# The gate and up products of both Swiglu layers by Strassen's recursion, seven products of 256 tokens in place of eight

## The chip, the cores and the metric

The kernel runs on one core of a Trainium2 chip. Its time is device microseconds (us) of one launch. All tensors are float32.

## The reference

Three blocks of different make follow one another on 512 tokens of width 1024 (a Mamba-2 block with an MLP, a block with RWKV-7 and sliding attention between two Swiglu layers, and a block with spatial gating, forgetting attention and convolutional feed-forward layers). The change is about the two Swiglu layers of the second block:

```
D_MODEL, SEQ, D_FF_2 = 1024, 512, 2816

def rms_norm(x, g, eps=RMS_EPS):
    y = xf * lax.rsqrt(jnp.mean(xf * xf, axis=-1, keepdims=True) + eps)
    return y * g

def swiglu(h, w_gate, w_up, w_down):
    return (jax.nn.silu(h @ w_gate) * (h @ w_up)) @ w_down

def second_block(x, ...):
    x = x + 0.5 * swiglu(rms_norm(x, ffn1_norm[l]), ffn1_w_gate[l], ffn1_w_up[l], ffn1_w_down[l])
    ...  # the two mixers
    x = x + 0.5 * swiglu(rms_norm(x, ffn2_norm[l]), ffn2_w_gate[l], ffn2_w_up[l], ffn2_w_down[l])
    return rms_norm(x, final_norm[l])
```

## The kernel before

Activations lie transposed, features on the 128 partitions and the 512 tokens along the free side, in blocks of 128 features: `resid` has 8 blocks, the hidden layer of a Swiglu 22. All matrices go through one pipeline, the class `Flow`. It cuts its matrices into **steps** of at most 128x1024 weights, numbered through in `Flow.steps`. A step's weights are loaded by SyncE into one of four ring slots (`RING`); the load of step g waits until TensorE is through with step g-4. ScalarE rounds them into a high part (`split_high`), VectorE subtracts it from the whole and gets the low part (`split_low`), and TensorE makes three products for each 128x128 tile of weights: high weights by low activations, low by high, high by high (`multiply`). The semaphore `products` counts what TensorE has done, `emptied` counts the banks of its results that were taken.

A Swiglu has three matrices. Gate and up have 22 steps each. A step is one output block: 8 tiles, 3 products each, 24 matmuls of 512 tokens. Down has 8 output blocks of 22 tiles, 528 matmuls. VectorE takes a gate block from its bank and multiplies it with the factor of the norm (`rg.factor`, L2257), ScalarE applies Silu (L2238); VectorE multiplies the up block with it (L2269), ScalarE rounds the hidden block (L2243), VectorE makes its low part (L2273). The order of work on each engine is the order in which `Swiglu.tensor`, `scalar` and `vector` issue it; each engine keeps to its order and halts at a wait, with all that stands behind it. GpSimd does nothing in this stage. `Handoff` makes the high and low parts of the activations ahead of the first matrix, from each finished block of `resid`.

In the profile's rows all weight and activation memory is called `arena`, and L1317 and L1325 are the lines of `split_high` and `split_low`, L1377 is TensorE's in `multiply`, and L1280 is SyncE's load. The first Swiglu (`middle_bank`) runs its gate and up from about 1274 to 1516 us, the second (`later_bank`) from about 2143 to 2390 us.

## Time and profile before

| | us |
|---|---|
| three runs | 3604.70, 3606.09 (the median), 3608.92 |
| span of the profiled execution | 3608.4 |
| TensorE busy | 3540.6 |
| VectorE busy | 2041.9 |
| ScalarE busy | 1534.2 |
| GpSimd busy | 322.6 |

The span goes from the first to the last instruction of one execution that was profiled. It has no time of its own beside its span here, and lies among the three runs. Busy times are shares of different stages, so what a change in one stage is worth has to be read from that stage.

### The profile page before, as it was taken

How to read it: one execution, taken by the hardware profiler on the slowest of the kernel's cores; microseconds unless marked ns; L12 is line 12 of the kernel's file. 1: busy time of each engine (PE TensorE's matmuls, PEld its weight loads, DVE VectorE, ACT ScalarE, POOL GpSimd, SP SyncE). 2: the span in 40 equal slices, each digit the busy share in tenths (PEclk: the TensorE clock that was granted, in tenths of full speed). 3: DMA queues.
4: the chain of work that ended last, by engine and by line, in shares of the span. 5: the costliest groups of instructions: out<-in, count | busy, mean ns of one | idle time of the engine just before them, and what ended most of it. 6: DMA issues, size and time to landing. Idle time of an engine off the chain costs nothing. (4 is left out here: it accounts for less than half of the span.)

```text
span 3608.4 us, 49456 instructions
## 1 busy us (share of the span) xinstructions
PE 3540.6 (98%) x20379; PEld 2918.3 (81%) x20379; DVE 2041.9 (57%) x2881; ACT 1534.2 (43%) x2459; POOL 322.6 (9%) x307
## 2 busy tenths in 40 slices
PE   8999999999999999999999999999999999999998
PEld 6888788888788888887778778888988887877887
DVE  5987687775534454446686663444364744355743
ACT  5674678543423332222553432233353323275322
POOL 3772000000000000002111000000000000043000
PEclk9999999999999999999999999999999999999999
DMA  6345644333333333333320233333223333411332
GB/s 204 99 135 172 200 129 144 113 95 94 88 94 99 94 94 100 96 94 96 95 76 3 77 100 95 98 94 105 88 82 94 97 97 94 139 50 51 96 96 86
DMA packets 597624, 365.34 MB, mean 101 GB/s; under 512 B 16887, under 2 KB 578887, under 8 KB 596887
## 3 DMA queue, kind: packets, MB, share of 16 engines
q1 hardware_dynamic: 592807, 350.43, 32.8%
q10 hardware_dynamic: 4592, 11.73, 0.8%
q8 instruction: 162, 2.65, 0.3%
q14 instruction: 63, 0.52, 0.1%
HBM read 345.70 MB, written 15.89 MB: 100 GB/s over the span
## 5 line engine op out<-in xcount | busy, mean ns | idle before, releaser
L1377 PE MATMUL later_bank<-arena 128*128 128x512 f32 (+1 forms) x6792 | 1435.6, 373 | 9.8 <-DVE arena L1325 6.6
L1377 PEld LDWEIGHTS later_bank<-arena 128*128 128x128 f32 x6792 | 1193.2, 188 | 246.0 <-DVE arena L1325 14.3
L1317 ACT ACTIVATE arena<-arena 128x1024 fp32r<-128x1024 f32 (+3 forms) x545 | 566.4, 1039 | 1529.4 <-PE later_bank L1377 751.0
L1377 PE MATMUL middle_bank<-arena 128*128 128x512 f32 x4896 | 1125.5, 391 | 1.9 <-DVE arena L1325 1.1
L1377 PEld LDWEIGHTS middle_bank<-arena 128*128 128x128 f32 x4896 | 915.8, 187 | 210.4 <-issue 12.8
L1325 DVE TENSOR_TENSOR arena<-arena 128x1024 fp32r<-128x1024 f32 (+2 forms) x547 | 662.3, 1211 | 542.7 <-ACT arena L1317 537.0
L1377 PE MATMUL front_bank<-arena 128*128 128x512 f32 (+3 forms) x1776 | 349.4, 356 | 6.9 <-DVE arena L1325 4.7
L1377 PEld LDWEIGHTS front_bank<-arena 128*128 128x128 f32 (+1 forms) x1776 | 290.7, 188 | 62.9 <-DVE arena L1325 7.6
L1570 POOL TENSOR_TENSOR arena<-arena 128x512 f32<-128x512 f32 x120 | 171.2, 1426 | 113.3 <-ACT arena L1882 96.9
L1377 PE MATMUL ssd_bank<-arena 128*128 128x512 f32 x576 | 144.3, 402 | 0.2 <-DVE arena L1325 0.2
L2039 DVE SCALAR_TENSOR_TENSOR arena<-front_bank,columns,arena 128x510 f32<-128x510 f32 (+1 forms) x224 | 126.7, 628 | 18.1 <-ACT arena L1809 16.5
L1377 PEld LDWEIGHTS ssd_bank<-arena 128*128 128x128 f32 x576 | 107.3, 190 | 23.3 <-issue 1.4
L3320 POOL MEMSET arena<- 128x512 f32 x1 | 0.5, 527 | 1340.6 <-PE middle_bank L1377 1340.6
L2068 DVE SCALAR_TENSOR_TENSOR front_bank<-arena,columns,front_bank 128x512 f32<-128x512 f32 x116 | 87.5, 754 | 3.9
L538 ACT ACTIVATE arena<-arena 128x128 f32<-128x128 f32 x240 | 76.0, 387 | 27.8 <-DMA arena<-scratch_cum 27.8
L2692 POOL TENSOR_SCALAR arena<-arena,small 128x128 f32<-128x128 f32 (+3 forms) x64 | 68.3, 1085 | 150.6 <-DVE small L2886 150.1
L1882 ACT ACTIVATE arena<-arena,columns 128x512 f32<-128x512 f32 x120 | 78.5, 717 | 3.7 <-POOLq L1571 2.3
L2559 ACT ACTIVATE arena<-arena 128x512 f32<-128x512 f32 x32 | 20.2, 632 | 111.7 <-DVEq L2590 111.7
L2595 DVE TENSOR_TENSOR arena<-later_bank,arena 128x512 f32<-128x512 f32 x32 | 22.1, 692 | 78.1 <-PE later_bank L1377 78.1
L910 PEld LDWEIGHTS branch_bank<-arena 64*64 64x64 f32 x1792 | 55.8, 135 | 9.7 <-issue 7.3
L910 PE MATMUL branch_bank<-arena 64*64 64x64 f32 x1792 | 61.1, 221 | 0.7 <-DVEq L1096 0.7
L2153 DVE TENSOR_TENSOR arena<-arena 128x512 f32<-128x512 f32 x63 | 43.8, 695 | 21.0 <-ACT arena L2137 15.6
(486 smaller groups left out, 3014.0 us busy)
## 6 DMA issues: line engine op xcount, KB each, us to landing
arena<-in_w_in SPq DMA_DIRECT2D x114, 512.0 KB, 3.8
arena<-in_ffn_w_gate SPq DMA_DIRECT2D x76, 512.0 KB, 3.7
arena<-in_ffn_w_up SPq DMA_DIRECT2D x76, 512.0 KB, 3.7
arena<-in_w_mlp SPq DMA_DIRECT2D x64, 512.0 KB, 3.9
arena<-in_w_ada SPq DMA_DIRECT2D x48, 512.0 KB, 6.2
arena<-in_ffn_w_down SPq DMA_DIRECT2D x48, 512.0 KB, 4.0
arena<-scratch_cum SPq DMA_DIRECT2D x64, 256.0 KB, 6.7
arena<-in_gm_w_in SPq DMA_DIRECT2D x32, 512.0 KB, 3.8
```

The costliest lines, as they stand in the source:

```text
L538: ins = act.activation(seg[:, k, c, :], seg[:, k, c, :], ACT.Relu, scale=-1.0, bias=cum[:, c, h:h + 1])
L910: ins_ = pe.matmul(out[p, block_of(h)], left[p, h, :], right[p, h, :], start=True, stop=True)
L1317: act.activation(self.high[q % self.AHEAD][:, 0:kb * cols], self.raw[self.slot(g)][:, 0:kb * cols], ACT.Copy).then_inc(self.high_done, 1)
L1325: dve.tensor_tensor(self.low[self.slot(g)][:, 0:kb * cols], self.raw[self.slot(g)][:, 0:kb * cols], self.high[q % self.AHEAD][:, 0:kb * co ...
L1377: ins = pe.matmul(out, still, moving, start=first and n_pass == 0, stop=last and n_pass == 2)
L1570: order.then(pool.tensor_tensor(self.u[:, b, :], self.u[:, b, :], self.prod[:, m % self.PRODUCTS, :], ALU.add))
L1882: act.activation(self.prod[:, p % self.PRODUCTS, :].rearrange("p (s t) -> p s t", s=NSEG), tap, ACT.Copy, scale=column(core, "conv_dw_w", ...
L2039: ins = dve.scalar_tensor_tensor(dst, src, w, dst, ALU.mult, ALU.add)
L2068: self.mark = order.tick(dve.scalar_tensor_tensor(sums, tap, w, sums, ALU.mult, ALU.add))
L2153: dve.tensor_tensor(rg.acc, rg.acc, rg.squares[n % 2], ALU.add).then_inc(self.added, 1)
L2595: dve.tensor_tensor(self.whole[:, n, :], flow.bank(up, n), self.whole[:, n, :], ALU.mult).then_inc(flow.emptied["dve"], 1)
L2692: pool.tensor_scalar(buf, buf, self.rden[:, m % NJ:m % NJ + 1], None, ALU.mult).then_inc(self.normed, 1)
```

## The change

Two output blocks of gate (or of up) are now one `PairWork`. Its weights (1024x256) are taken as four pairs of input blocks, and each pair with its two output blocks as a 2x2 matrix of 128x128 tiles; the activations of the pair with the two halves of the 512 tokens are a 2x2 matrix of 128x256 tiles. The product of the two 2x2 matrices is made with seven tile products in place of eight (the form of Winograd, with four sums of weights, four of activations and seven of results). A pair has two steps, each with 7 results x 2 pairs of input blocks x 3 matmuls = 42 matmuls of 256 tokens. There are 11 gate pairs and 11 up pairs in a Swiglu, 44 in all, which now take turns (gate 0, up 0, gate 1, ...).

- GpSimd makes the four weight sums of each step (`sum_weights`: four operations of 128x256, three results into extra tiles and one in the place of a weight tile), and it multiplies a gate pair with the norm factor (128x1024).
- ScalarE rounds 1024 weights and 768 sums of a step, VectorE makes the low parts of both. There are three buffers for high parts in these steps.
- Seven banks hold the seven results. ScalarE copies the first (`copy_first`), VectorE adds up the four output quarters in five operations (`combine`). TensorE may write a bank of the next pair when `emptied` says that it was taken (banks 1 to 6 after operation 1, 2, 4, 3, 5, 5 of `combine`).
- `PairHandoff` makes the four activation sums on VectorE, then high and low parts of seven tiles for each pair of blocks.
- Down is cut in two: the first eight hidden blocks are multiplied after gate pair 4 (`downs[0]`, 8 steps), the others at the end (16 steps of 7 tiles). The residual is updated in both. The matmuls of down stay 528.

```diff
@@ class PairWork (new) and Flow @@
+class PairWork:
+    PARTS, PER, PRODUCTS = 2, 2, 7
+
+    def __init__(self, w, x, n, ready=None):
+        self.w, self.x, self.ready = w[:, 2 * P * n:2 * P * (n + 1)], x, ready
+        self.plain, self.pair, self.cols, self.units, self.by = False, True, 2 * P, 1, "pair"
+        self.cuts = (2 * self.PER,) * self.PARTS
+        self.parts = self.steps = self.PARTS
+        self.first_row = [2 * self.PER * n for n in range(self.PARTS)]
...
+            if j.pair:
+                j.index, j.opens = pairs, held[0:j.PRODUCTS]
+                held[0:j.PRODUCTS] = [("first", pairs + 1)] + [("pair", 5 * pairs + n) for n in (1, 2, 4, 3, 5, 5)]
+                pairs += 1
+                for s in range(j.steps):
+                    g = len(self.steps)
+                    self.splits_before.append(len(self.split_steps))
+                    self.split_steps.append(g)
+                    self.take_high(used_high, 3, g)
+                    self.sums_index[g] = len(self.sums_order)
+                    self.sums_order.append(g)
+                    self.steps.append((j, s))
+                    count += 1
+                    self.unit_after.append(count)
+                j.unit_done[0] = count
+                continue
...
+    def take_high(self, used, count, g):
+        at = min(range(count), key=lambda b: used[b])
+        self.high_at.append(at)
+        self.high_after.append(used[at])
+        used[at] = g
...
+            r = self.sums_index[g]
+            act.wait_ge(self.summed, 4 * (r + 1))
+            act.activation(high, self.raw[self.slot(g)][:, 0:kb * cols], ACT.Copy)
+            if r >= len(self.sums_high):
+                act.wait_ge(self.products, self.unit_after[self.sums_order[r - len(self.sums_high)] + 1])
+            act.activation(self.sums_high[r % len(self.sums_high)], self.sums[r % len(self.sums)], ACT.Copy).then_inc(self.high_done, 1)
...
+            rest = dve.tensor_tensor(low, raw, self.high[self.high_at[q]][:, 0:kb * cols].bitcast(F32), ALU.subtract)
+            if g in self.sums_index:
+                r = self.sums_index[g]
+                at = r % len(self.sums)
+                rest = dve.tensor_tensor(self.sums_low[at], self.sums[at], self.sums_high[r % len(self.sums_high)].bitcast(F32), ALU.subtract)
+            rest.then_inc(self.low_done, 1)
...
+    def sum_weights(self, pool, last):
+
+        while self.next_sum < len(self.sums_order) and self.sums_order[self.next_sum] <= last:
+            r, g = self.next_sum, self.sums_order[self.next_sum]
+            self.next_sum += 1
+            self.wait_landed(pool, g)
+            if r >= len(self.sums):
+                pool.wait_ge(self.products, self.unit_after[self.sums_order[r - len(self.sums)] + 1])
+            a21, a11, a22, a12 = (self.raw[self.slot(g)].rearrange("p (n s c) -> p s n c", s=4, c=P)[:, i, :, :] for i in range(4))
+            s1, s2, s3 = (self.sums[r % len(self.sums)].rearrange("p (s n c) -> p s n c", s=3, c=P)[:, i, :, :] for i in range(3))
+            pool.tensor_tensor(s1, a21, a22, ALU.add).then_inc(self.summed, 1)
+            pool.tensor_tensor(s3, a11, a21, ALU.subtract).then_inc(self.summed, 1)
+            pool.wait_ge(self.summed, 4 * r + 2)
+            pool.tensor_tensor(s2, s1, a11, ALU.subtract).then_inc(self.summed, 1)
+            pool.wait_ge(self.summed, 4 * r + 3)
+            pool.tensor_tensor(a21, a12, s2, ALU.subtract).then_inc(self.summed, 1)
+
+    def multiply_pair(self, pe, j):
+
+        for part in range(j.parts):
+            g = j.step0 + part
+            q, r = self.splits_before[g], self.sums_index[g]
+            self.wait_low(pe, q)
+            plain = [b.rearrange("p (n s c) -> p s n c", s=4, c=P) for b in (self.high[self.high_at[q]], self.low[self.slot(g)])]
+            sums = [b.rearrange("p (s n c) -> p s n c", s=3, c=P) for b in (self.sums_high[r % len(self.sums_high)], self.sums_low[r % len(self.sums)])]
+            products = ((plain, 1, 0), (sums, 1, 6), (sums, 2, 5), (sums, 0, 4), (plain, 3, 2), (plain, 2, 1), (plain, 0, 3))
+            order = [(at, n) for at in range(j.PRODUCTS) for n in range(j.PER)]
+            if j.ready:
+                order.sort(key=lambda it: it[1])
+            for at, n in order:
+                (w, slot, moving), k = products[at], part * j.PER + n
+                first, last = k == 0, k == j.parts * j.PER - 1
+                if j.ready and at == 0:
+                    j.ready(pe, k)
+                if first and j.opens[at]:
+                    by, count = j.opens[at]
+                    pe.wait_ge(self.emptied[by], count)
+                w_high, w_low = (b[:, slot, n, :] for b in w)
+                x_high, x_low = (x[:, moving, :] for x in j.x(k))
+                for n_pass, (still, x) in enumerate(((w_high, x_low), (w_low, x_high), (w_high, x_high))):
+                    ins = pe.matmul(self.banks[at][:, 0:TC], still, x, start=first and n_pass == 0, stop=last and n_pass == 2)
+                if last and at in (0, 1, 3, 4):
+                    ins.then_inc(self.pair_banks, 1)
+            ins.then_inc(self.products, 1)
+
+    def copy_first(self, act, j, out):
+
+        act.wait_ge(self.pair_banks, 4 * j.index + 1)
+        act.activation(out[:, 2, :], self.banks[0][:, 0:TC], ACT.Copy).then_inc(self.emptied["first"], 1)
+
+    def combine(self, dve, j, out):
+
+        emptied, done = self.emptied["pair"], 5 * j.index
+        sides = out[:, 0:4:3, :]
+        dve.wait_ge(self.emptied["first"], j.index + 1)
+        dve.wait_ge(self.pair_banks, 4 * j.index + 2)
+        dve.tensor_tensor(out[:, 1, :], out[:, 2, :], self.banks[1][:, 0:TC], ALU.add).then_inc(emptied, 1)
+        dve.wait_ge(emptied, done + 1)
+        dve.wait_ge(self.pair_banks, 4 * j.index + 3)
+        dve.tensor_tensor(sides, out[:, 1:2, :].to_broadcast([P, 2, TC]), self.all_banks[:, 2:4, 0:TC], ALU.add).then_inc(emptied, 1)
+        dve.wait_ge(self.pair_banks, 4 * j.index + 4)
+        dve.tensor_tensor(out[:, 2, :], out[:, 2, :], self.banks[4][:, 0:TC], ALU.add).then_inc(emptied, 1)
+        dve.wait_ge(emptied, done + 2)
+        dve.tensor_tensor(out[:, 1, :], out[:, 0, :], self.banks[3][:, 0:TC], ALU.add).then_inc(emptied, 1)
+        dve.wait_ge(emptied, done + 4)
+        self.wait_product(dve, j, 0)
+        dve.tensor_tensor(sides, sides, self.all_banks[:, 5:7, 0:TC], ALU.add).then_inc(emptied, 1)
@@ class PairHandoff (new) and Swiglu @@
+    def round(self, act, k):
+        act.wait_ge(self.x_summed, 4 * (k + 1))
+        act.activation(self.x_high[:, k], self.x[:, k], ACT.Copy).then_inc(self.high_done, 1)
+
+    def rest(self, dve, k):
+        dve.wait_ge(self.high_done, 3 * (k + 1))
+        dve.tensor_tensor(self.x_low[:, k], self.x[:, k], self.x_high[:, k].bitcast(F32), ALU.subtract).then_inc(self.low_done, 1)
+
+    def vector(self, dve, n):
+        k, half = divmod(n, 2)
+        if n and half == 0:
+            self.rest(dve, k - 1)
+        b11, b12, b21, b22, t1, t3, t2 = (self.x[:, k, i, :] for i in range(self.SLOTS))
+        order = self.order = Order(dve, self.x_summed) if n == 0 else self.order
+        dve.wait_ge(self.high_done, n + 1 + n // 2)
+        if half == 0:
+            order.tick(dve.tensor_tensor(t1, b12, b11, ALU.subtract))
+        else:
+            order.wait(order.n)
+            order.tick(dve.tensor_tensor(t2, b22, t1, ALU.subtract))
+            order.then(dve.tensor_tensor(t3, b22, b12, ALU.subtract))
+            order.tick(dve.tensor_tensor(b12, b21, t2, ALU.subtract))
+        self.add_squares(dve, n)
+        if n == DB - 1:
+            self.rest(dve, k)
...
-        self.gate = Work(w_gate, [self.operand], (DB,), P, by="dve", ready=self.wait_operand)
-        self.up = Work(w_up, [self.operand], (DB,), P, by="dve")
...
+        self.gates = [PairWork(w_gate, x, p, ready=None if p else lambda pe, k: self.into.wait(pe, k)) for p in range(pairs)]
+        self.ups = [PairWork(w_up, x, p) for p in range(pairs)]
+        first = 2 * self.FIRST_PAIRS
+        self.downs = [Work(w_down[at * P:(at + sum(cuts)) * P, :], [lambda k, at=at: (self.high[:, self.block(at + k), :], self.low[:, self.block(at + k), :])],
+                           cuts, P, by="dve", ready=lambda pe, k, at=at: pe.wait_ge(*self.low_done((at + k) // 2)))
+                      for at, cuts in ((0, (first,)), (first, (7, 7)))]
+        for j in self.downs:
+            j.banks = (7, *range(7))
+        self.down = self.downs[1]
+        self.products = []
+        for p in range(pairs):
+            ahead = p == self.FIRST_PAIRS
+            self.products += [(self.gates, p)] + [(self.downs, 0)] * ahead + [(self.ups, p)]
+        self.products.append((self.downs, 1))
+        self.jobs = [kind[p] for kind, p in self.products]
...
+    def pool(self, pool):
+        rg, flow = self.rg, self.flow
+        flow.sum_weights(pool, self.gates[0].step0 + 4)
+        for kind, p in self.products:
+            if kind is self.downs:
+                continue
+            s = kind[p].step0
+            flow.sum_weights(pool, min(s + 5, self.jobs[-1].step0))
+            if kind is self.gates:
+                pool.wait_ge(self.into.ready, 1)
+                flow.wait_combined(pool, kind[p])
+                whole = self.pair(p, self.whole)
+                pool.tensor_tensor(whole, whole, rg.factor.unsqueeze(1).to_broadcast([P, 2, T]), ALU.mult).then_inc(self.scaled, 1)
+            flow.sum_weights(pool, min(s + 6, self.jobs[-1].step0))
...
     def vector(self, dve):
+        rg, resid, flow, into = self.rg, self.rg.core.resid, self.flow, self.into
+        before = into.before
+        flow.split_low(dve, flow.ahead(self.gates[0].step0))
+        for kind, p in self.products:
+            j = kind[p]
+            if kind is self.downs:
+                self.add_down(dve, order, j)
+                continue
+            flow.combine(dve, j, self.target(kind, p))
+            if kind is self.gates:
+                if p == 0:
+                    into.inverse(dve)
+                elif p == 1 and before:
+                    dve.wait_ge(into.rooted, 2)
+                    order.then(dve.reciprocal(before.first, before.squares[0]))
+                flow.split_low(dve, flow.ahead(j.step0 + 1))
+            else:
+                whole = self.pair(p, self.whole)
+                flow.wait_combined(dve, j)
+                dve.wait_ge(*self.silu_done(p))
+                dve.tensor_tensor(whole, whole, self.other, ALU.mult).then_inc(self.hidden_by_vector, 1)
+                flow.split_low(dve, flow.ahead(j.step0 + 1))
+                dve.wait_ge(*self.high_done(p))
+                dve.tensor_tensor(self.pair(p, self.low), whole, self.pair(p, self.high).bitcast(F32), ALU.subtract).then_inc(self.hidden_by_vector, 1)
+            flow.split_low(dve, min(flow.ahead(j.step0 + 2), self.next_pair(j)))

```

GpSimd's program in the first Swiglu, after the sums of the first five steps. `arena1` to `arena4` are the ring's slots, `arena12` the sums, `arena107` the gate pair and `arena91` the norm factor. Before, nothing stood here:

```order
L1417 TENSOR_TENSOR arena12<-arena3 128x256
L1418 TENSOR_TENSOR arena12<-arena3 128x256
L1420 TENSOR_TENSOR arena12<-arena12,arena3 128x256
L1422 TENSOR_TENSOR arena3<-arena3,arena12 128x2x128
L2476 TENSOR_TENSOR arena107<-arena107,arena91 128x1024
L1417 TENSOR_TENSOR arena12<-arena4 128x256
L1418 TENSOR_TENSOR arena12<-arena4 128x256
L1420 TENSOR_TENSOR arena12<-arena12,arena4 128x256
L1422 TENSOR_TENSOR arena4<-arena4,arena12 128x2x128
```

New are the four sums of each step and, after a gate pair, the factor between the sums of two steps.

VectorE's program in the up product of the first Swiglu before. `arena103` is the hidden block, `arena105` and `arena104` its high and low part, `middle_bank` the up result; `arena1` to `arena8` are the ring's slots (whole and low), `arena9` and `arena10` the high weights:

```order
L2269 TENSOR_TENSOR arena103<-middle_bank2,arena103 128x512
L1325 TENSOR_TENSOR arena6<-arena2,arena9 128x1024
L2273 TENSOR_TENSOR arena104<-arena103,arena105 128x512
L2269 TENSOR_TENSOR arena103<-middle_bank3,arena103 128x512
L1325 TENSOR_TENSOR arena7<-arena3,arena10 128x1024
```

The result of a block is taken with one operation, and one step of weights is split for each.

The same engine now, from the `combine` of an up pair to the first operation of the `combine` of the next gate pair (`arena110` is the up pair, `arena107` the gate pair and then the hidden one, L1395 and L1399 are the low parts of the weights and of their sums):

```order
L1463 TENSOR_TENSOR arena110<-arena110,middle_banks 128x256
L1466 TENSOR_TENSOR arena110<-arena110,middle_banks 128x2x256
L1468 TENSOR_TENSOR arena110<-arena110,middle_banks 128x256
L1470 TENSOR_TENSOR arena110<-arena110,middle_banks 128x256
L1473 TENSOR_TENSOR arena110<-arena110,middle_banks 128x2x256
L2559 TENSOR_TENSOR arena107<-arena107,arena110 128x1024
L1395 TENSOR_TENSOR arena8<-arena4,arena11 128x1024
L1399 TENSOR_TENSOR arena13<-arena12,arena14 128x768
L2562 TENSOR_TENSOR arena108<-arena107,arena109 128x1024
L1395 TENSOR_TENSOR arena5<-arena1,arena9 128x1024
L1399 TENSOR_TENSOR arena13<-arena12,arena14 128x768
L1463 TENSOR_TENSOR arena107<-arena107,middle_banks 128x256
```

The last split before the next L1463 is that of a step whose ring slot was still in use at the end of the pair whose results are combined above (step0 + 5 of that pair, in the slot of its second step).

## Rows read from the trace of the kernel before

**Rows 1.** The page, part 1: busy time, share of the span, instructions of each engine.

```profile
PE 3540.6 (98%) x20379; PEld 2918.3 (81%) x20379; DVE 2041.9 (57%) x2881; ACT 1534.2 (43%) x2459; POOL 322.6 (9%) x307
```

**Rows 2.** Windows, gate and up of the first Swiglu.

```profile
core 0: us, PE busy (x) PEld busy (x) DVE busy (x) ACT busy (x) POOL busy (x), PEclk, DMA share, GB/s
1270.00:1516.00 246.00, 245.48 (x1079) 202.04 (x1078) 111.91 (x125) 76.30 (x96) 0.00 (x0) 1.00 0.33 95
```

**Rows 3.** Line L2269, the 22 up blocks of the second Swiglu: durations min/median/max, first and last start.

```profile
L2269 DVE TENSOR_TENSOR arena<-later_bank,arena x22: 691/692/692, 2270.1 to 2384.4; 128x512 f32<-128x512 f32 x22
```

**Rows 4.** Timeline of TensorE, matmuls of 256 tokens in the spatial gating: start, us.

```profile
2568.99 31.92 PE L1377 MATMUL later_bank<-arena 128*128 128x256 f32 x264
2600.75 1.02 PE L2357 MATMUL later_bank<-arena,mean_of_width 128*128 128x512 f32 x2
```

**Rows 5.** DMA issues by source: KB each, median us from issue to landing.

```profile
arena<-in_ffn_w_up SPq DMA_DIRECT2D x76, 512.0 KB, 3.7
```

**Rows 6.** Timeline of GpSimd, operations that nothing holds up.

```profile
1643.94 0.46 POOL L740 TENSOR_TENSOR arena<-arena 128x128 f32<-128x128 f32 x1
94.41 1.29 POOL L1570 TENSOR_TENSOR arena<-arena 128x512 f32<-128x512 f32 x1 [0.18 <-POOL arena L1570]
```

**Rows 7.** Groups by line and shape of ScalarE and VectorE: busy us, mean ns | idle before.

```profile
L1317 ACT ACTIVATE arena<-arena 128x1024 fp32r<-128x1024 f32 x495 | 524.7, 1060 | 1399.5 <-PE later_bank L1377 689.0 <-PE middle_bank L1377 574.2 <-DMA arena<-in_w_in 81.9
L1317 ACT ACTIVATE arena<-arena 128x896 fp32r<-128x896 f32 x32 | 30.5, 953 | 102.4 <-PE middle_bank L1377 53.3 <-PE later_bank L1377 49.1
L1325 DVE TENSOR_TENSOR arena<-arena 128x896 fp32r<-128x896 f32 x32 | 34.8, 1089 | 29.7 <-ACT arena L1317 29.7
L654 DVE TENSOR_TENSOR arena<-arena,ssd_bank 128x256 f32<-128x256 f32 x24 | 10.1, 422 | 3.7 <-PE ssd_bank L486 1.3
L2181 DVE RECIPROCAL arena<-arena 128x512 f32<-128x512 f32 x6 | 20.1, 3353 | 13.7 <-ACT arena L2173 13.7
```

**Rows 8.** Timelines of ScalarE, VectorE, the up product: one step.

```profile
2302.75 1.06 ACT L1317 ACTIVATE arena<-arena 128x1024 fp32r<-128x1024 f32 x1 [3.86 <-PE later_bank L1377]
...
2302.76 0.69 DVE L2269 TENSOR_TENSOR arena<-later_bank,arena 128x512 f32<-128x512 f32 x1 [2.53 <-PE later_bank L1377]
2303.84 1.23 DVE L1325 TENSOR_TENSOR arena<-arena 128x1024 fp32r<-128x1024 f32 x1 [0.39 <-ACT arena L1317]
2304.99 0.69 DVE L2273 TENSOR_TENSOR arena<-arena 128x512 fp32r<-128x512 f32 x1
```

**Rows 9.** Timelines of VectorE and GpSimd in the first stage, where both work.

```profile
91.33 1.76 DVE L1325 TENSOR_TENSOR arena<-arena 128x1024 fp32r<-128x1024 f32 x1
93.01 3.12 DVE L2068 SCALAR_TENSOR_TENSOR front_bank<-arena,columns,front_bank 128x512 f32<-128x512 f32 x4
96.03 1.22 DVE L1325 TENSOR_TENSOR arena<-arena 128x1024 fp32r<-128x1024 f32 x1
...
90.71 1.29 POOL L1570 TENSOR_TENSOR arena<-arena 128x512 f32<-128x512 f32 x1 [0.51 <-ACT arena L1882]
92.18 2.05 POOL L1570 TENSOR_TENSOR arena<-arena 128x512 f32<-128x512 f32 x1 [0.18 <-POOL arena L1570]
96.13 2.27 POOL L1570 TENSOR_TENSOR arena<-arena 128x512 f32<-128x512 f32 x1 [0.43 <-ACT arena L1882]
```

**Rows 10.** Timelines of GpSimd and VectorE in the mixer.

```profile
1646.84 1.35 POOL L740 TENSOR_TENSOR arena<-arena 128x128 f32<-128x128 f32 x1
...
1646.65 1.23 DVE L1325 TENSOR_TENSOR arena<-arena 128x1024 fp32r<-128x1024 f32 x1
```

**Rows 11.** Waits of TensorE, the longest kinds: us, times, longest us.

```profile
PE later_bank L1377 <- DVE arena L1325: 6.6, 13, 1.0
PE branch_bank L881 <- DVE arena L1063: 4.8, 1, 4.8
```

337 lines of the change are left out of this document (213 added, 124 removed).

## The prediction

> **What bounds the kernel now.** I read the page's busy shares first: TensorE is busy 98% of the span, all others at most 57% [rows 1]. Then the window of gate and up of one Swiglu: TensorE works 245.5 of 246.0 us at a granted clock of 1.00 (the 2.4 GHz level), VectorE 111.9, ScalarE 76.3, GpSimd not at all [rows 2]. The waits say the same: TensorE waits for VectorE's low parts 6.6 us in 13 pieces in the whole last stage [rows 11]. So this stage is a row of matmuls without holes, and what is to be read is the pace of one step: 22 up blocks start 5.443 us apart ((2384.4 - 2270.1) / 21) [rows 3]. A step has 24 matmuls, 0.2268 us each. Two steps, the work of one new pair, take 10.89 us. There are 44 such pairs.
>
> **The term that is removed.** The spatial gating has matmuls of 256 tokens that also load new weights each time: 264 of them fill 31.76 us (2568.99 to 2600.75), 0.1203 us each [rows 4]. That is 53% of a long one, not half. A pair has 84: 10.1 us instead of 10.89. If everything else hides, the change is worth 44 x 0.78 = 34 us. The Trainium skill ("TensorE: Matmul & The Clock Gate", Back-to-back issue gap) gives columns / 2.4 GHz plus some 2.5 ns. By it a pair would go from 10.4 to 9.2 us, worth 53 us; the trace does not agree (0.1203, not 0.109), so I keep the row.
>
> **What is added, and the loop that it closes.** Before, the chain from a freed ring slot to the split weights had much room: ScalarE idles 3.86 us of each step for TensorE [rows 8]. Now I follow one slot. Pair j ends at E_j. Then
>
> - the load of the step with number step0 + 5 is issued into the slot of the pair's second step: 3.7 us to landing [rows 5];
> - GpSimd makes four sums of 128x256. A 128x128 operation takes 0.46 us, a 128x512 one 1.29, with 0.18 of idle time between dependent ones [rows 6]. A third of the way between them is 0.74; with two dependent gaps the step takes 3.3 us. The ends are 0.46 and 1.29 an operation (2.2 and 5.5 us); both rows are adds and products of two float32 tiles, so I stay close to the line between them, 0.68 to 0.80;
> - ScalarE rounds 1024 and 768 columns: 1.06 and 0.85 (a 128 columns shorter one takes 0.107 less) [rows 7], 1.9 us;
> - VectorE makes both low parts: 1.23 [rows 8] and 0.95 (1.089 for 896, so 0.136 less for each 128) [rows 7], 2.2 us. From the end on ScalarE to the start on VectorE is 0.03 us [rows 8]; four handovers add 0.1.
>
> Sum without any hindrance: L = 11.2 us. In `Swiglu.vector` this split stands in front of the `combine` of pair j+1, and VectorE keeps its order. So the banks of pair j+1 are given back only after E_j + L. Pair j+2 starts at E_(j+1), about 10.1 us after E_j. It can write the first bank, but the second needs `combine`'s first operation, the third the second and the fourth the fourth; the four take 0.42 + 0.69 + 0.42 + 0.42 = 1.95 us (256 columns 0.422 [rows 7], 512 columns 0.69 [rows 8]) and TensorE reaches the fourth bank 18 matmuls, 2.2 us, after its start. The waits inside `combine` use up the rest, so they cancel. That gives E_(j+2) = max(E_(j+1), E_j + L) + 10.1, and over two pairs a mean of (L + 10.1) / 2 each. Where L is over 10.1, TensorE waits for banks. What is late next is nothing else: the load, the sums and the splits of the later steps all hang on the same ends.
>
> **The port.** In the first stage VectorE and GpSimd both work on two memory operands, and the trace shows that they don't do so together. GpSimd's addition starts at 90.71, VectorE's split at 91.33 takes 1.76 instead of 1.22 and ends at 93.09; GpSimd's next addition starts at 92.18, takes 2.05 instead of 1.29 and ends 1.14 after the split did. One starting with a split takes 2.27 [rows 9], and a small one 1.35 instead of 0.46 [rows 6, 10]. The operations at 93.01 with a bank as an operand delay nobody (GpSimd's 1.29 at 94.41 [rows 6]). So a split costs GpSimd 0.76 to 0.98 us if it meets one, 0.87 in the mean, and the one of 768 columns 0.59. In L, the four sums meet the two low parts of the step before (in the order of VectorE they come at the same time, 4 to 8 us after E_j): + 1.5 us. Two low parts each wait for about half of a GpSimd operation: + 0.5. L = 13.2 us and a pair takes 11.65 in the mean.
>
> The Trainium skill ("SBUF — State Buffer", Who interferes with whom) has a rule against this change: a VectorE instruction with two SBUF inputs and a GpSimd instruction that reads SBUF exclude each other, and the second waits for the whole of the first. The trace agrees in kind, but a delay of 0.53 where the rest of the GpSimd instruction was 0.67 (92.00 - 91.33) shows that it lets go earlier. By the rule the sum would be that of the last rival below.
>
> **The sum.** The pairs come in two runs, 9 (gate 0 to gate 4) and 13 (up 4 to up 10). The first pair of each is not held, since no `combine` stands before it: 2 x 10.1 + 20 x 11.65 = 253.2 us for a Swiglu, against 22 x 10.89 = 239.6. That is +13.6 for each and +27 us for both. Other parts, at nothing:
>
> - The down products are the same 528 matmuls; during `downs[0]` VectorE has per step a scaling, two residual operations and a split, 0.75 + 0.69 + 0.69 + 1.23 = 3.4 of 5.4 us (each is within 0.1 of a 512-column or split row [rows 7, 8]).
> - The activation sums at the entry lengthen the way from the last block of `resid` to its low part (rounding and splitting 1792 columns, 1.7 and 2.0 us by the same slopes, and three sums, 1.3) to about 7 us. TensorE has 63 matmuls, 7.6 us, on the other blocks first. If that cover fails: 2 us for each Swiglu.
> - The factor's reciprocal, 3.35 us on VectorE [rows 7], comes right after the first `combine` and delays one split, whose load is the later one anyway.
>
> The profiled span, 3608.4, goes to 3635.6; the runs' median lies 2.3 us lower, 3606.1. It goes to **3633 us**. Below 0.2% (7 us) a measurement of this kernel can't tell a change.
>
> **Rivals.**
>
> 1. *The operations miss each other on the port.* The low parts fall into GpSimd's idle time. L stays 11.2, a pair 10.65: 2 x (20.2 + 213.0 - 239.6) = -13 us, 3593. For it: most GpSimd rows of the first stage have the plain 1.29. Against it: GpSimd has 4 x 3.3 + 2.4 (the 1024-column factor) = 15.6 us of work for two pairs, of some 21 to 23. The point at which it decides: L below 11.7 is faster than before.
> 2. *All hides.* If L is at most 10.1, because a GpSimd operation of 256 columns costs nearer to 0.46, TensorE stays full: -34 us, 3572.
> 3. *No change that can be told*: L near 11.7, a pair 10.9.
> 4. *GpSimd becomes the bound.* Held up by every one of VectorE's ten two-operand instructions in two pairs (6 of 1.23, 4 of 0.95 us, + 7.6 us) it needs 15.6 + 0.5 + 7.6 = 23.7 us, 11.9 a pair: +37 us, still the forecast's range. If each holds the port for its whole length, it is 14.2 of its own instructions and 11.2 of VectorE's, 12.7 a pair: 2 x (20.2 + 254 - 239.6) = +69 us, 3675.
>
> **How the numbers follow.** Forecast 0.55, rival 1 0.15, rival 2 0.10, rival 3 0.10, rival 4 at +69 0.10. The forecast's own range is L from 12.0 (collisions half as many) to 14.5 (GpSimd's operation at 0.80 and its factor in the way): 11.05 to 12.3 a pair, +3 to +53, 3609 to 3659. The range goes down to rival 1 with some room and up to the end of the forecast: 3586 to 3662. It leaves out rival 2 and most of rival 4. Faster 0.25, same 0.10, slower 0.65.
>
> **What would show it.** After the change, TensorE's 256-token matmuls should still have 0.12 us where they run unbroken. In every pair but the first of a run TensorE should wait for VectorE at the second to fourth bank (line L1447, released by L1463 to L1470), about 1.5 us a pair in the mean and 3 us in every other one. GpSimd's sums should have two lengths, near 0.74 and 1.4 to 1.7 us, and be busy over 80% of the stage. The last split before `combine` should end 13 us after a pair's end. Wrong would be: TensorE full (then the loop is shorter than its rows), waits for L1395/L1399 in place of banks (then GpSimd is the bound), or a granted clock below 1.00 in these stages, which no term here has.

## The result, and the profile after

The change makes the kernel slower: median 3715.41 us (3708.55 to 3718.78, 4 runs) against 3605.39 (3604.59 to 3608.92, 4 runs), a ratio of 1.0299, 95% interval 1.0287 to 1.0312. I had forecast 3633, with a range of 3586 to 3662. The direction was right, the size was not: the change costs 110 us and I had 27. The profiled execution has a span of 3710.9 us against 3608.4, 102.5 more.

The page of the changed kernel, part 1, answers to [rows 1]:

```profile
PE 3556.3 (96%) x21963; PEld 3005.8 (81%) x21963; DVE 2327.7 (63%) x3157; ACT 1617.7 (44%) x2553; POOL 755.1 (20%) x681
```

TensorE's busy time should have fallen by 44 x 0.78 = 34 us. It rose by 16. So its matmuls themselves became slower, and that is not seen in any wait. The windows of the same stage as [rows 2] say how:

```profile
core 0: us, PE busy (x) PEld busy (x) DVE busy (x) ACT busy (x) POOL busy (x), PEclk, DMA share, GB/s
1270.00:1516.00 246.00, 219.49 (x1480) 206.08 (x1480) 189.36 (x189) 86.92 (x105) 149.26 (x130) 0.92 0.29 82
```

TensorE stands still for 26.5 us of 246, and its granted clock is 0.92, where it was 1.00: in this stretch the 2.4 GHz level is not granted all the time. The waits of TensorE over the whole kernel, the six largest kinds (us, times, longest), answer to [rows 11]:

```profile
PE later_banks L1447 <- DVE arena L1463: 19.1, 12, 2.1
PE later_banks L1528 <- DVE arena L1395: 17.6, 15, 3.1
PE middle_banks L1447 <- DVE arena L1463: 16.7, 11, 2.0
PE middle_banks L1447 <- ACT arena L1455: 13.2, 8, 2.3
PE middle_banks L1528 <- DVE arena L1395: 11.0, 5, 4.2
PE later_banks L1447 <- ACT arena L1455: 9.5, 6, 1.8
```

L1447 are the new products, L1463 is the first operation of `combine`, L1455 is `copy_first`. The L1463 rows are the bank waits that the prediction names; that the first bank would be waited for too, because ScalarE's copy is late, it did not say. The L1528 rows are different: they are waits of the plain products (MLP, join, down) for a low part. The same two kinds were 6.6 and 1.1 us before.

A steady piece of the second Swiglu, timeline of TensorE:

```profile
2432.73 0.95 PE L1447 MATMUL later_banks<-arena 128*128 128x256 f32 x6 [1.66 <-ACT arena L1455]
2435.45 21.18 PE L1447 MATMUL later_banks<-arena 128*128 128x256 f32 x162 [1.77 <-DVE arena L1463]
2458.20 0.95 PE L1447 MATMUL later_banks<-arena 128*128 128x256 f32 x6 [1.56 <-ACT arena L1455]
2460.92 21.18 PE L1447 MATMUL later_banks<-arena 128*128 128x256 f32 x162 [1.78 <-DVE arena L1463]
```

and the window of that one cycle:

```profile
2435.45:2460.90 25.45, 22.13 (x168) 21.75 (x168) 20.57 (x20) 9.59 (x13) 18.26 (x18) 0.93 0.29 84
```

One cycle, two pairs (168 matmuls), is 2460.92 - 2435.45 = 25.5 us: 3.3 of waits and 22.1 of matmuls. Before, the same work was 21.78. The waits stand before every second pair, at its first and its second bank. The forecast had 23.3: 3.1 of waits and 20.2 of matmuls. The slow matmuls stand right behind the pauses: from 2435.45 to 2440.45 the granted clock is 0.66 and 29 matmuls take 5.00 us, and from 2440.45 to the end of the cycle it is 1.00.

The chain behind one wait, timelines in that cycle: GpSimd, what VectorE does meanwhile, ScalarE, and VectorE after it:

```profile
2450.37 0.74 POOL L1417 TENSOR_TENSOR arena<-arena 128x256 f32<-128x256 f32 x1 [1.91 <-DMA arena<-in_ffn_w_up]
2451.07 1.72 POOL L1418 TENSOR_TENSOR arena<-arena 128x256 f32<-128x256 f32 x1
2452.86 1.33 POOL L1420 TENSOR_TENSOR arena<-arena 128x256 f32<-128x256 f32 x1
2454.28 1.60 POOL L1422 TENSOR_TENSOR arena<-arena 128x256 f32<-128x256 f32 x1
...
2450.40 1.79 DVE L1395 TENSOR_TENSOR arena<-arena 128x1024 fp32r<-128x1024 f32 x1 [0.86 <-ACT arena L1383]
2452.11 1.49 DVE L1399 TENSOR_TENSOR arena<-arena 128x768 fp32r<-128x768 f32 x1
2453.52 1.75 DVE L2562 TENSOR_TENSOR arena<-arena 128x1024 fp32r<-128x1024 f32 x1
...
2455.99 1.06 ACT L1380 ACTIVATE arena<-arena 128x1024 fp32r<-128x1024 f32 x1 [4.67 <-POOL arena L1422]
2456.96 0.82 ACT L1383 ACTIVATE arena<-arena 128x768 fp32r<-128x768 f32 x1
2457.69 0.36 ACT L1455 ACTIVATE arena<-later_banks 128x256 f32<-128x256 f32 x1
...
2457.81 1.33 DVE L1395 TENSOR_TENSOR arena<-arena 128x1024 fp32r<-128x1024 f32 x1 [2.54 <-ACT arena L1383]
2459.06 1.47 DVE L1399 TENSOR_TENSOR arena<-arena 128x768 fp32r<-128x768 f32 x1
2460.46 0.41 DVE L1463 TENSOR_TENSOR arena<-arena,later_banks 128x256 f32<-128x256 f32 x1
```

Read it from the top. The load lands and GpSimd makes four sums in 5.5 us instead of 3.3, and three of them run beside two-operand operations of VectorE: the low parts of the step before (L1395, L1399) and the low part of the hidden pair (L2562). Then come 1.8 us of rounding and 2.7 of splitting. Only then comes `combine`, for banks whose products had long been done; the short copy at 2457.69 had stood behind the rounding. With 3.7 us for the load the loop is about L = 13.8 (the forecast had 13.2).

The stages outside the steady cycles are the other half. TensorE at the start of the first Swiglu:

```profile
1243.78 22.34 PE L1528 MATMUL middle_banks<-arena 128*128 128x512 f32 x96 [2.09 <-DVE arena L1395]
1270.35 8.64 PE L1528 MATMUL middle_banks<-arena 128*128 128x512 f32 x24 [4.23 <-DVE arena L1395]
1278.82 5.19 PE L1447 MATMUL middle_banks<-arena 128*128 128x256 f32 x42
1289.79 6.95 PE L1447 MATMUL middle_banks<-arena 128*128 128x256 f32 x42 [5.78 <-DVE arena L1399]
...
1297.03 10.63 PE L1447 MATMUL middle_banks<-arena 128*128 128x256 f32 x84
```

The last output block of the MLP waits 4.23 us for its weights' low part, the second half of the first pair 5.78 us for that of its own step, and the 24 matmuls in between take 8.64 us where 24 x 0.2268 = 5.4 are needed (the granted clock is 0.81 from 1264 to 1290 us). The first pair takes 18.2 us (1278.82 to 1297.03) instead of 10.1.

### The profile page after: what moved, and what is told of

Its sections match the earlier page's. It is cut to its first block and busy times, and to the rows that moved or that the text cites. A ratio compares the mean times of both kernels' runs of the same rounds, so it can differ in the third digit from the quotient of the medians.

```text
span 3710.9 us, 53586 instructions
## 1 busy us (share of the span) xinstructions
PE 3556.3 (96%) x21963; PEld 3005.8 (81%) x21963; DVE 2327.7 (63%) x3157; ACT 1617.7 (44%) x2553; POOL 755.1 (20%) x681
## 5 line engine op out<-in xcount | busy, mean ns | idle before, releaser
L1528 PE MATMUL later_banks<-arena 128*128 128x512 f32 (+2 forms) x5736 | 1201.2, 371 | 20.8 <-DVE arena L1395 17.6
L1528 PEld LDWEIGHTS later_banks<-arena 128*128 128x128 f32 (+1 forms) x5736 | 998.4, 189 | 217.1 <-DVE arena L1395 25.9
L1395 DVE TENSOR_TENSOR arena<-arena 128x1024 fp32r<-128x1024 f32 (+2 forms) x547 | 689.9, 1262 | 519.5 <-ACT arena L1376 418.9
L1528 PE MATMUL middle_banks<-arena 128*128 128x512 f32 (+1 forms) x3840 | 889.5, 393 | 11.8 <-DVE arena L1395 11.0
L1528 PEld LDWEIGHTS middle_banks<-arena 128*128 128x128 f32 (+1 forms) x3840 | 719.3, 188 | 180.2 <-DVE arena L1395 16.2
L1528 PE MATMUL front_bank<-arena 128*128 128x512 f32 (+3 forms) x1776 | 350.0, 357 | 3.8 <-DVE arena L1395 3.0
L1528 PEld LDWEIGHTS front_bank<-arena 128*128 128x128 f32 (+1 forms) x1776 | 291.1, 188 | 59.7 <-issue 6.4
L1417 POOL TENSOR_TENSOR arena<-arena 128x256 f32<-128x256 f32 x88 | 81.7, 929 | 1249.1 <-DMA arena<-in_ffn_w_gate 1096.4
L1447 PE MATMUL later_banks<-arena 128*128 128x256 f32 x1848 | 245.3, 297 | 34.7 <-DVE arena L1463 19.1
L1447 PE MATMUL middle_banks<-arena 128*128 128x256 f32 x1848 | 243.6, 296 | 35.7 <-DVE arena L1463 16.7
L1447 PEld LDWEIGHTS later_banks<-arena 128*128 128x128 f32 x1848 | 240.4, 205 | 39.9 <-DVE arena L1463 21.5
L1447 PEld LDWEIGHTS middle_banks<-arena 128*128 128x128 f32 x1848 | 238.4, 203 | 41.1 <-DVE arena L1463 19.1
L1528 PE MATMUL ssd_bank<-arena 128*128 128x512 f32 x576 | 144.9, 403 | 0.2 <-DVE arena L1395 0.2
L2191 DVE SCALAR_TENSOR_TENSOR arena<-front_bank,columns,arena 128x510 f32<-128x510 f32 (+1 forms) x224 | 126.7, 627 | 18.3 <-ACT arena L1961 16.4
L1399 DVE TENSOR_TENSOR arena<-arena 128x768 fp32r<-128x768 f32 x88 | 137.5, 1563 | 0.0
L1528 PEld LDWEIGHTS ssd_bank<-arena 128*128 128x128 f32 x576 | 107.6, 190 | 23.4 <-issue 1.4
L1422 POOL TENSOR_TENSOR arena<-arena 128x256 f32<-128x256 f32 x88 | 101.6, 1155 | 6.9
```

The costliest lines, as they stand in the source:

```text
L1395: rest = dve.tensor_tensor(low, raw, self.high[self.high_at[q]][:, 0:kb * cols].bitcast(F32), ALU.subtract)
L1399: rest = dve.tensor_tensor(self.sums_low[at], self.sums[at], self.sums_high[r % len(self.sums_high)].bitcast(F32), ALU.subtract)
L1417: pool.tensor_tensor(s1, a21, a22, ALU.add).then_inc(self.summed, 1)
L1422: pool.tensor_tensor(a21, a12, s2, ALU.subtract).then_inc(self.summed, 1)
L1447: ins = pe.matmul(self.banks[at][:, 0:TC], still, x, start=first and n_pass == 0, stop=last and n_pass == 2)
L1528: ins = pe.matmul(out, still, moving, start=first and n_pass == 0, stop=last and n_pass == 2)
```

## The experiments

All times below are medians. The kernel before ran beside each group, with 3605.96, 3605.61 and 3607.81 us.

**1. The split moved behind `combine`.** If the loop is the cause, it can be opened by order alone.

```diff
             flow.combine(dve, j, self.target(kind, p))
+            if late is not None:
+                flow.split_low(dve, late)
+                late = None
...
-            flow.split_low(dve, min(flow.ahead(j.step0 + 2), self.next_pair(j)))
+            late = min(flow.ahead(j.step0 + 2), self.next_pair(j))
+            if self.products[at + 1][0] is self.downs:
+                flow.split_low(dve, late)
+                late = None
```

and the same on ScalarE, behind `copy_first`.

> Edit: within a Swiglu the last pair of splits after a product of two blocks (ScalarE's high part and VectorE's low part of the weights of step0+5) is moved behind the next product's first copy on ScalarE and behind its five combining operations on VectorE, where that next product is another pair. All sums, splits and matmuls stay. Theory A (the loop: load 3.7 us, GpSimd sums 3.3, high 1.9, low 2.2, standing ahead of the next pair's combining, is what holds TensorE for 3.3 us in every 25.45 us, and these waits are what lowers its granted clock to 0.90 to 0.94): both go. A pair then takes 10.1 to 10.9 us instead of 12.7, over 40 held pairs that is 72 to 104 us less than the 3715 of the changed kernel: 3610 to 3645 us. Rival B (VectorE and GpSimd are simply too busy, and their SBUF accesses lock each other out, so that a pair costs about 12 us in whatever order): the waits move to another line, the time stays within 15 us of 3715. Rival C (the granted clock falls because of the mix of 256-token matmuls itself, not the waits): the 3.3 us of waits go, the clock stays at 0.92: some 66 us less at most from waits, none from the clock, 3650 to 3665.

Measured: 3658.0 us (3655.4 to 3660.48), ratio 1.0146 (1.0131 to 1.0162), 57 us less than the change. The window of the second run of pairs in the first Swiglu:

```profile
1441.00:1604.00 163.00, 153.13 (x1148) 146.38 (x1146) 134.06 (x140) 66.70 (x82) 122.55 (x96) 0.99 0.33 94
```

The clock is back at 0.99 and the steady cycle is 21.8 us (1524.11 to 1545.92, between two waits of one kind). So the loop was real, and the low clock went with its waits. The time lies in C's range, but not by C's mechanism, which kept the clock at 0.92. It is above A's range because the cycle went to 21.8 us and not to 20.2, and because the ends of the stages, which this edit does not touch, cost more than I thought. In this order GpSimd is busy 75% of the stretch (122.55 of 163), and what TensorE waits for is mostly the low part of the weight sums (L1399).

**2. The sums without their reads.** GpSimd keeps four operations a step, but only writes, and the kernel leaves out the values of the weight sums.

```diff
-            pool.tensor_tensor(s1, a21, a22, ALU.add).then_inc(self.summed, 1)
-            pool.tensor_tensor(s3, a11, a21, ALU.subtract).then_inc(self.summed, 1)
-            pool.wait_ge(self.summed, 4 * r + 2)
-            pool.tensor_tensor(s2, s1, a11, ALU.subtract).then_inc(self.summed, 1)
-            pool.wait_ge(self.summed, 4 * r + 3)
-            pool.tensor_tensor(a21, a12, s2, ALU.subtract).then_inc(self.summed, 1)
+            for n in range(4):
+                if n:
+                    pool.wait_ge(self.summed, 4 * r + n)
+                pool.memset(self.sums[r % len(self.sums)], 0.3).then_inc(self.summed, 1)
```

> Edit: GpSimd's four sums of each step are replaced by four writes of a constant into the tile of sums, 128x768 each (about 0.73 us each by the 0.84 us of 896 elements), so GpSimd is busy as long as before but reads nothing of SBUF while VectorE works. Leaves out the values of the weight sums. Theory A (of the loop's 14.4 us, 25.45 less a pair's 11.05, about 2 to 3 us are VectorE's and GpSimd's two-operand operations waiting for each other): GpSimd's operations fall from means of 0.93 to 1.16 us to about 0.75, the cycle of two pairs falls from 25.45 to 22 to 23.5 us, 40 to 70 us less: 3645 to 3675. Rival B (no contention to speak of; the durations overlap by chance and the order alone counts): within 15 us of 3715.

Measured: 3621.5 us (3618.98 to 3622.36), ratio 1.0043 (1.0027 to 1.0060), 94 us less than the change, more than theory A had. The order of the instructions is that of the change, so the loop is still closed. Timelines of GpSimd and VectorE, one step:

```profile
1503.01 3.14 POOL L1418 MEMSET arena<- 128x768 f32 x4 [1.90 <-DMA arena<-in_ffn_w_up]
...
1508.09 1.23 DVE L1395 TENSOR_TENSOR arena<-arena 128x1024 fp32r<-128x1024 f32 x1 [1.55 <-ACT arena L1383]
1509.23 0.95 DVE L1399 TENSOR_TENSOR arena<-arena 128x768 fp32r<-128x768 f32 x1
1510.10 0.42 DVE L1459 TENSOR_TENSOR arena<-arena,middle_banks 128x256 f32<-128x256 f32 x1
```

From the landing to `combine` (here L1459) it is 7.1 us, with the load's 3.7 L = 10.8. TensorE's restarts lie 21.2 us apart (1521.28 to 1542.46), and L plus a pair of 10.1 us is 20.9. So the formula of the prediction holds at a second point. The price of the reads meeting each other is 13.8 - 10.8 = 3 us in a cycle like the one above, where I had 2.0. In the traces the 42 pairs behind the first one of each Swiglu take 523.8 us in the change and 445.4 here. Of these 78 us, 32 are TensorE's busy time (464.0 and 431.6: mostly the clock, which is 1.00 here) and 46 its waits. The profiled executions differ by 91.0 us; the other 13 lie at the ends of the stages. The edit also changes the values that TensorE multiplies, so this run alone does not show that the pauses lower the clock; the next one does.

**3. TensorE kept busy while it waits.**

```diff
+                if first and at < 2 and j.fill:
+                    for _ in range(j.fill):
+                        pe.matmul(self.banks[7][:, 0:TC], j.x(0)[0][:, 0, 0:P], j.x(0)[0][:, 0, :], start=True, stop=True)
                 if first and j.opens[at]:
```

with `fill` 12 for the up pairs but two. The extra products go nowhere.

> Edit: before each of the two waits for banks at the start of an up pair (products 0 and 1; not for the first and the fifth pair) TensorE does 12 extra matmuls of 256 tokens into bank 7, whose results nobody reads: 1.44 us each time, 2.9 us of the 3.3 us in which it stands still in each 25.45. Theory A (the granted clock of 0.90 to 0.94 comes from these waits): the clock returns to 0.98 to 1.00, the useful matmuls of two pairs take 20.2 to 20.6 us instead of 22.1, and the time falls by 20 x 2 x 1.5 to 1.9, less what the fillers add beyond the waits (up to 0.4 us per cycle): 3640 to 3665 us. Rival B (the clock has another cause, or the cycle is set by VectorE, GpSimd and the loads alone, so that faster matmuls only wait longer): the clock rises or not, but the time stays at 3705 to 3720. Rival C (fillers come on top, since the wait that they precede does not shrink): up to 3750.

Measured: 3687.87 us (3685.42 to 3690.7), ratio 1.0230 (1.0214 to 1.0245), 27.5 us less than the change, with 432 more matmuls. Two cycles in the second Swiglu:

```profile
2440.41 1.60 PE L1444 MATMUL later_banks<-arena 128*128 128x256 f32 x12
2442.09 0.98 PE L1451 MATMUL later_banks<-arena 128*128 128x256 f32 x6
2442.91 1.60 PE L1444 MATMUL later_banks<-arena 128*128 128x256 f32 x12
2444.95 19.71 PE L1451 MATMUL later_banks<-arena 128*128 128x256 f32 x162 [0.45 <-DVE arena L1467]
```

The 162 useful matmuls take 19.71 us, not 21.18, and a cycle takes 24.1 (2420.88 to 2444.95) instead of 25.5. Nothing on VectorE, GpSimd or the queues was changed. So the slower matmuls of the change are a result of TensorE's pauses, and they do cost time: 1.4 us a cycle, 28 us in 20. That is theory A's mechanism, at 23 us above its range, since I had counted 1.5 to 1.9 us for each pair and not for each cycle of two. Rivals B and C fall.

**4. The activations rounded earlier.** ScalarE rounds a pair of blocks in the handoff to the Swiglu ahead of a split of weights that used to stand before it.

```diff
-        if n and half == 0:
-            self.round(act, k - 1)
...
-        if n == DB - 1:
+        if half:
             self.round(act, k)
```

> Edit: in the handoff of activations to a Swiglu, ScalarE rounds a pair of blocks (with their sums) directly after its squares of the odd block instead of at the start of the next even block, ahead of the split of weights that stands between. Nothing else. Theory A (the product before each Swiglu ends 5.1 and 8.2 us late because VectorE's rest waits for this rounding, queued behind ScalarE's split, and the split of weights for TensorE comes late behind that): a part of these 13.3 us and of the 15.8 us that the two first pairs lose comes back, 4 to 20 us: 3695 to 3711. Rival B (those stages are late because GpSimd's and VectorE's operations lengthen each other, wherever the rounding stands; or ScalarE now waits for the activations' sums instead, ahead of the split): within 4 us of 3715, or up to 10 us slower.

Measured: 3695.84 us (3684.98 to 3703.6), ratio 1.0249 (1.0226 to 1.0272), 20 us less than the change, inside theory A's range. The end of the MLP:

```profile
1242.26 22.35 PE L1528 MATMUL middle_banks<-arena 128*128 128x512 f32 x96 [0.25 <-DVE arena L1395]
1266.08 5.75 PE L1528 MATMUL middle_banks<-arena 128*128 128x512 f32 x24 [1.48 <-DVE arena L1395]
1271.67 5.19 PE L1447 MATMUL middle_banks<-arena 128*128 128x256 f32 x42
1282.63 7.76 PE L1447 MATMUL middle_banks<-arena 128*128 128x256 f32 x42 [5.77 <-DVE arena L1399]
```

The waits of 2.09 and 4.23 us are 0.25 and 1.48 now, the 24 matmuls take 5.75 and not 8.64, and the Swiglu starts at 1271.67 instead of 1278.82: 7.1 us for this entry. The 5.77 of the first pair stay. In this kernel the steady cycles have the same waits as the changed one, but some go at full clock. Windows of three cycles in a row:

```profile
1487.00:1511.80 24.80, 21.62 (x168) 21.24 (x168) 20.11 (x21) 9.28 (x13) 17.90 (x17) 0.95 0.29 86
1511.80:1535.75 23.95, 20.65 (x169) 20.27 (x169) 20.38 (x21) 9.61 (x13) 18.67 (x18) 1.00 0.30 88
1535.75:1559.65 23.90, 20.64 (x168) 20.26 (x169) 20.33 (x21) 9.60 (x13) 18.45 (x18) 1.00 0.31 89
```

So a cycle at 1.00 is 23.9 us and one at 0.93 is 25.5. That is the price of the clock a second time, with nothing filled in; the changed kernel has one such cycle too (1544.51 to 1568.49, 24.0 us at 1.00). It fits the scatter of this kernel's runs by 19 us: the two near 3688 us have a mean granted clock of 0.986, the two near 3702 have 0.982 and 0.981. The traces say where the gain lies, 22.0 us between the profiled executions: 7.1 at the first entry, 7.9 between the first Swiglu's last pair and the end of the product before the second Swiglu (591.4 us in the change, 583.5 here), and 6.7 in the pairs behind the first one of each Swiglu, by the clock.

**5. Both orders together** (experiments 1 and 4).

> Edit: the later place of the last splits (as in the run with the moved splits, 3658 us) and the earlier rounding of the activations (3696 us) together. If they act at different places (steady pairs, and the ends of the stages before them) the gains of 57 and 20 us add: 3633 to 3645. If the earlier rounding mostly shifted the pairs' waits so that the clock recovered in some of them (its trace has some pairs at full rate, 162 matmuls in 19.7 us), it adds only 3 to 10 us: 3648 to 3656.

Measured: 3651.3 us (3649.04 to 3652.64), ratio 1.0127 (1.0112 to 1.0142), 7 us less than experiment 1. They don't add. At the first entry the trace has 9.5 us less than experiment 1 (the Swiglu starts at 1270.03 us, not at 1279.54). Between the two Swiglus some of it is lost, in a stage that no edit touches. Windows of the same 150 us of the mixers, experiment 1 and this one:

```profile
1900.00:2050.00 150.00, 145.03 (x3068) 126.23 (x3064) 92.47 (x181) 59.55 (x164) 23.54 (x21) 0.98 0.01 3
1890.00:2040.00 150.00, 147.39 (x3006) 128.32 (x3004) 93.24 (x181) 58.20 (x163) 23.54 (x21) 0.93 0.01 3
```

From TensorE's first product behind the first Swiglu to the last part of the product before the second it takes 468.0 us here (1653.63 to 2121.65) and 462.6 in experiment 1 (1663.55 to 2126.17). The earlier rounding then wins 5.5 us back in that product, and the first pair of the second Swiglu takes 2.7 more. The time lies in the expectation's second range, but the trace does not show the reason given there: the 42 pairs behind the first one of each Swiglu take 469.5 us here and 469.3 in experiment 1, so no clock of theirs is at play, and in experiment 4 itself 15 of the 22 us came from the entries. Why the mixers go at 0.93 in this kernel is open.

**6. The moved splits, and the sums without their reads.**

> Edit: the later place of the last splits, and GpSimd's sums replaced by as many constant writes of 128x768 (the values of the weight sums are left out). Theory A (order and contention for SBUF are all that holds the steady pairs): a pair takes 10.1 to 10.3 us, and only the entries are left, 13 to 20 us over the bound of 3572: 3585 to 3605 us. Rival B (something else, such as the loads' landing 3.7 us after a product, still holds them): no more than 5 us below the 3621.5 of the run with constant writes alone.

Measured: 3608.27 us (3602.81 to 3613.18, 10 runs), ratio 1.0008 (0.9999 to 1.0018), 13 us less than experiment 2 and 50 less than experiment 1; 3 us above theory A's range. The 13 pairs of the second run are one row now:

```profile
1424.02 131.47 PE L1443 MATMUL middle_banks<-arena 128*128 128x256 f32 x1092
```

That is 131.47 / 13 = 10.11 us a pair, the 10.1 of the prediction. The steady part is as good as it can be, and still the kernel is only level with the one before. So the ends of the stages cost as much as Strassen's recursion saves, some 35 us.

**7. A fifth sum in every step.** One more `pool.tensor_tensor(s2, a21, a22, ALU.add)` ahead of the four, in the order of the change.

> Edit: one more GpSimd sum of 128x256 in each step of the changed kernel (five instead of four, the extra one overwritten at once); 0.74 us alone, up to 1.6 beside VectorE. Theory A (GpSimd's sums stand in the loop that holds the steady pairs, once per two pairs, and lengthen VectorE's splits): each cycle of two pairs grows by 0.8 to 2.5 us, over 20 cycles 16 to 50 us, some more in the first pairs and by a lower clock: 3735 to 3775. Rival B (GpSimd already fills the cycle: four steps of sums per two pairs): 4 x 0.9 to 1.5 us per cycle, 72 to 120 us more: 3787 to 3835. Rival C (GpSimd is off the path): within 6 us of 3715.

Measured: 3727.46 us (3725.23 to 3728.55), ratio 1.0337 (1.0320 to 1.0354), 12 us more than the change, below theory A's range. The steady cycle did not grow at all: 25.4 us (1529.70 to 1555.08). The last step's sums, timeline of GpSimd:

```profile
1544.65 0.73 POOL L1417 TENSOR_TENSOR arena<-arena 128x256 f32<-128x256 f32 x1
1545.35 0.73 POOL L1418 TENSOR_TENSOR arena<-arena 128x256 f32<-128x256 f32 x1
1546.04 0.74 POOL L1419 TENSOR_TENSOR arena<-arena 128x256 f32<-128x256 f32 x1
1546.85 1.60 POOL L1421 TENSOR_TENSOR arena<-arena 128x256 f32<-128x256 f32 x1
1548.53 1.33 POOL L1423 TENSOR_TENSOR arena<-arena 128x256 f32<-128x256 f32 x1
```

Five sums take 5.2 us, four had taken 5.5. With one more sum before it VectorE's split came later, and only two sums met one in place of three. So the price of GpSimd's work depends on which operations fall together: in the steady cycle one more operation cost nothing. I had taken it as a sum. The kernel's 12 us (15.9 in the profiled execution) lie elsewhere: the first Swiglu starts 3.9 us later (1282.68) and its two runs of pairs take 2.8 and 3.6 us more. GpSimd is busy 89% of the stretch from 1441 to 1604 us here, 69% in the change.

**8. GpSimd relieved.** Experiment 5, and the gate's product with `rg.factor` (128x1024, mean 3.3 us on GpSimd in the window of the second run) moved to VectorE:

```diff
-                pool.tensor_tensor(whole, whole, rg.factor.unsqueeze(1).to_broadcast([P, 2, T]), ALU.mult).then_inc(self.scaled, 1)
...
+                dve.wait_ge(into.ready, 1)
+                flow.wait_combined(dve, j)
+                dve.tensor_tensor(whole, whole, rg.factor.unsqueeze(1).to_broadcast([P, 2, T]), ALU.mult).then_inc(self.scaled, 1)
```

> Edit: as the first of these four, and the gate's product with the factor of its tokens (128x1024 with a second operand from SBUF, mean 3.05 us on GpSimd) moved to VectorE, where such an operation took 1.2 to 1.8 us, behind the splits that follow a gate product's combining. GpSimd's own work falls from 15.7 to 13.3 us in two pairs, VectorE's rises from 16.4 to 17.6. Theory A (with the splits moved, GpSimd beside VectorE is the bound: about 22 us of a cycle): 0.5 to 1.2 us per two pairs less, 10 to 24 us below the first of these four: 3615 to 3630 if that gives 3638. Rival B (VectorE is the bound): 5 to 25 us above it.

Measured: 3622.12 us (3620.72 to 3630.02), ratio 1.0051 (1.0036 to 1.0066), 29 us less than experiment 5. Theory A, by more than its 24: with the splits moved, GpSimd beside VectorE is the bound, and an operation of 2.4 us or more on GpSimd takes 1.7 on VectorE. In the traces 20.7 us of it lie in those 42 pairs (469.5 to 448.8).

**9. One split earlier at the entry.** In the MLP's last step VectorE splits the Swiglu's second step of weights before it waits for the last output block.

```diff
             for s in range(down.steps):
+                if half and s == down.steps - 1:
+                    flow.split_low(dve, down.step0 + s + 2)
                 for n in flow.blocks(down, s):
```

> Edit: the version at 3622 us (splits moved, earlier rounding, the factor's product on VectorE), and in the product before the first Swiglu VectorE makes the low part of the Swiglu's second step of weights before it waits for the last output block, not after the handoff of that block. In the trace of that version TensorE waits 5.77 us for this low part in the first pair. Theory A (only its place makes it late): the wait shrinks to what the activations of the last block leave, about 3.3 us, the time falls by 2 to 3 us: 3619 to 3620. Rival B: the handoff of the last block, now 0.5 us or more later, moves the wait to itself: within 1 us of 3622.

Measured: 3621.9 us (3616.55 to 3623.4, 6 runs), ratio 1.0032 (1.0020 to 1.0044) against 1.0051. The intervals overlap, so the total alone does not settle it. TensorE at the entry:

```profile
1271.43 7.71 PE L1447 MATMUL middle_banks<-arena 128*128 128x256 f32 x63
1280.85 2.77 PE L1447 MATMUL middle_banks<-arena 128*128 128x256 f32 x21 [1.71 <-DVE arena L2382]
...
1287.34 9.62 PE L1447 MATMUL middle_banks<-arena 128*128 128x256 f32 x78 [2.15 <-DVE arena L1463]
```

The wait of 5.77 us became one of 1.71 for the activations of the last block, and 2.15 of it came back in the next pair. The first two pairs end some 3 us sooner than in experiment 8, counted from the Swiglu's start.

**10. Experiment 8 with the sums without their reads.**

> Edit: the version at 3622 us with GpSimd's sums replaced by as many constant writes of 128x768 (the values of the weight sums are left out). Theory A (what holds the steady pairs of that version at 21.5 us for two is the two engines' reads of SBUF lengthening each other): two pairs take 20.2 us, 20 x 1.3 = 26 us less, and a few us at the entries: 3588 to 3597, below the kernel before but 15 us or more above the 3572 of a change that hides wholly; that rest is what the entries of the activations cost. Rival B (VectorE's own work is the bound, 17.6 us alone in two pairs with its waits): at most 10 us less: 3612 to 3622.

Measured: 3594.31 us (3593.46 to 3596.71, 5 runs), ratio 0.9959 (0.9947 to 0.9972). This is the only version faster than the kernel before, and it leaves the weight sums out. It is theory A: a pair takes 10.1 us, and 28 us are gone against experiment 9 (24 of them in the 42 pairs, by the traces). It still lies 22 us above the 3572 of a change that hides wholly. No version that leaves nothing out beat the kernel before; the best, experiments 8 and 9, are 0.3 to 0.5% slower. Of the 14 to 17 us that they are behind, 3 to 5 lie in the mixers, which take 468.0 and 466.2 us in their traces, at the same clock of 0.93, against 462.9 before.

## Why the prediction was wrong in size

**Right.** The direction. The pace of the new matmuls where they run unbroken (0.1203 us forecast; 131.47 / 1092 = 0.1204 in experiment 6). The loop, its members and its place: TensorE waits at the first banks of every second pair, 3.3 us a cycle where I had 3.1. About half of it stands before the first bank, for ScalarE's copy (L1455); I had said that TensorE can write that bank at once. Single costs: a sum of 0.74 us, the rounding of 1.06 and 0.83, the low parts of 1.23 and 0.95. The formula (L + pair) for two pairs: shown by experiment 2 at L = 10.8, and by the cycles of experiment 4 at a clock of 1.00, 23.9 us for 13.8 + 10.1. That the meeting of reads is what makes the change slower than before: with them taken away and the order kept, only 0.43% are left of 2.99.

**The term that was left out: the clock.** "84 matmuls x 0.1203" was used for held pairs too. The trace shows 22.1 us for two pairs and not 20.2, at a granted clock of 0.90 to 0.94. Experiments 3 and 4 show the price: 1.4 to 1.5 us a cycle, 28 to 30 us in 20 cycles. The prediction named a granted clock below 1.00 as what would show it wrong, and gave it no term.

**The term costed at nothing: the entries and the downs.** "If that cover fails: 2 us for each Swiglu." It fails by far more. From the trace of the change: the product before the Swiglu ends 5.3 us late in the first and 8.2 in the second; the first pairs take 18.2 and 18.8 us instead of 10.1 each; each `downs[0]` is preceded by a wait of 1.99, and the second one takes 1.6 longer than the first (45.25 and 43.65, at clocks of 0.96 and 1.00); and from the last down product of the second Swiglu on there are seven waits for a low part of a plain step that sum to 7.6 us (2400 to 2700 us), where before they summed to 2.6. That is 13.5 + 16.8 + 4.0 + 1.6 + 5.0 = 41 us. The cause at the first entry is shown in part (experiments 4 and 9): a queue on ScalarE and one on VectorE, in which the activations' longer handoff and the weights' splits stand in each other's way. I had followed the activations' own way (7 us against a cover of 7.6) but not what is queued behind it on the same engines. In experiments 4 and 8 the first product of the layer starts 7.1 and 6.4 us sooner than in the change. For the second entry there is only the earlier rounding: it takes the waits of 1.49 and 3.10 us out of the product before, but leaves 2.55 us before the first pair (experiments 4 and 5).

**The term that was too small: the port.** I had + 2.0 us for L, it is about + 2.6 in the cycle shown (5.5 for 3.3 at the sums, 2.7 for 2.2 at the low parts); experiment 2 gives 3 against its own chain. I had let the four sums meet two low parts; they meet a third operation, the low part of the hidden pair, which costs the last sum 0.86 us (1.60 for 0.74). Over 20 such cycles that would be 12 us. The Trainium skill ("SBUF — State Buffer", Who interferes with whom) says that a VectorE instruction with two SBUF inputs contends with a GpSimd instruction that reads SBUF, and not with one that only writes, and that one with at most one SBUF input, outside the 2-port modes, does not contend. All three stand in the traces: L1399 goes from 0.95 to 1.47 beside the sums, is 0.95 beside the writes of experiment 2, and L1463, with a bank as one operand, has 0.41 or 0.42 in both.

Together: the 42 pairs behind the first one of each Swiglu took 523.8 us where the forecast had 40 x 11.65 + 2 x 10.1 = 486.2, 38 more. The clock has 28 to 32 of them (20 cycles, or TensorE's busy time against experiment 2), which leaves 6 to 10 for the port and not 12: in the first nine pairs of the second Swiglu a cycle is 24.8 us (2227.78 to 2252.57). With the 41 of the entries and the downs that is 79 us, against a miss of 3710.9 - 3635.6 = 75 us in the profiled execution. The terms are read from different places of the trace and can overlap by a few us.

**Slips in the prediction's sums.** They change nothing here. With two pairs of each Swiglu not held, the L below which the change is faster is 11.8 by the prediction's own sum (20.2 + 10 x (L + 10.1) = 239.6), not 11.7. The range's upper end, 3662, is 3 us over the forecast's own 3659.

**The rivals.** Rivals 1, 2 and 3 needed an L of 11.2, of at most 10.1 and of about 11.7; it was 13.8. Rival 1 (the operations miss each other) would have been luck in the timing: experiment 7 shows that a shift by one operation changes how many meet, and in the change they did meet. GpSimd is busy 72% of a cycle (18.3 of 25.5 us), not over 80% as the forecast said, and rival 4's 3675 by a saturated GpSimd did not come to be. Something near rival 4 bounds the kernel once the loop is open: in experiment 1 TensorE waits for L1399, the sign that the prediction gave for it, and experiments 8 and 10 shorten the pairs by relieving GpSimd or its reads.

**Open.** Why the last down product of the second Swiglu waits 0.97 us at most of its output blocks, with or without the sums' reads, was not tried. Nor was the port tried with the sums on another engine. Why the same mixers go at a clock of 0.93 in experiments 5, 8 and 9 and at 0.97 to 0.99 in the others is not known.

## What to carry to other kernels

When a change puts an engine into the loop that feeds TensorE, price three things and not one: the wait itself, the lower clock of the matmuls behind it (here 1.5 us beside 3.3 us of waits), and the ends of the stage, where the same engines also carry the handoff. Before moving work to GpSimd, add up the two-operand SBUF work of VectorE and GpSimd together (here 11.2 and 15.6 us alone in a cycle of 20.2). Each alone fits into the cycle, the two together don't, and none of the orders tried here hid them. A saving of 7% of a stage that runs without holes needs its cover proven at the first and last steps too.

## What the runs showed of the hardware that was not expected

Two pauses of TensorE of 1.6 and 1.8 us with six matmuls between them, once in 25 us, went with a granted clock of 0.90 to 0.94; with the pauses filled but for 0.45 us it was at 1.00 (experiment 3); with pauses of the same length it was 1.00 in some cycles too (experiment 4, 23.9 us instead of 25.5). Behind a pause of 4.23 us at a stage's end 24 matmuls took 8.64 us in the change and 7.11 in experiment 7; they take 5.75 in experiment 4. So the same pause did not always cost the same.

The clock can change in a stage that the edit leaves alone: over the same 150 us of the mixers it was 0.97 before, 0.99 in the change and 0.93 in experiments 5, 8 and 9, and the stage took 462.9, 461.0 and 466.2 to 468.0 us. When two edits don't add, the untouched stages have to be read too.

Four dependent writes of 128x768 on GpSimd take 3.14 us, and neither they nor VectorE's two-operand operations beside them grow; four dependent sums of 128x256 take 3.2 us alone (2445.25 to 2448.46 in the change) and 5.5 beside VectorE (2450.37 to 2455.88).
